# Strassen groups for all of an FFN, with the sums of its weight blocks made in DRAM

## The reference, cut to what matters

```python
h = rms_norm(x, g_pre_ffn)
x = x + rms_norm((silu(h @ w_gate) * (h @ w_up)) @ w_down, g_post_ffn)
```

## Time and profile before

| | us |
|---|---|
| median of 3 runs | 1280.83 |
| lowest and highest | 1280.55, 1282.76 |
| the profiled execution | 1281.71 |
| its span | 1279.6 |

### The profile page before, as it was taken

One profiled execution on the slowest core, in us unless ns is written; L12 is line 12 of the kernel. 1 busy time (PEld: TensorE's weight loads), 2 busy tenths in 40 slices (PEclk: granted clock), 3 DMA queues, 4 the chain that ended last, 5 costly groups with the idle time before them and its releaser, 6 DMA issues.

```text
span 1279.6 us, 16976 instructions
## 1 busy us (share of the span) xinstructions
PE 1270.1 (99%) x6329; PEld 1061.1 (83%) x6329; DVE 761.4 (60%) x1554; ACT 594.1 (46%) x1239; POOL 49.9 (4%) x97
## 2 busy tenths in 40 slices
PE   9999999999999999999999999999999999999998
PEld 8887777898888888888888888788878788999987
DVE  4366776654555455547675678675545534976664
ACT  5366676543453345335453324563335542463533
POOL 1010100100000000000100010000000000000000
PEclk9999999999999999999999999999999999999999
DMA  6279894222252236232525898212221022353531
GB/s 249 99 214 257 241 263 141 70 99 99 99 198 99 99 122 222 85 132 99 171 94 173 243 273 238 77 67 99 99 99 67 33 99 100 125 195 125 197 133 66
DMA packets 31937, 181.01 MB, mean 141 GB/s; under 512 B 3944, under 2 KB 4204, under 8 KB 12784
## 3 DMA queue, kind: packets, MB, share of 16 engines
q1 hardware_dynamic: 24360, 141.19, 31.6%
q0 software_dynamic: 4608, 33.56, 10.3%
q10 hardware_dynamic: 2888, 5.18, 1.2%
HBM read 171.52 MB, written 37.76 MB: 164 GB/s over the span
## 4 chain that ended last, share of the span: by engine, by line
PE 95%; DVE 1%; DMA 1%; issue 1%; POOL 0%; ACT 0%; ACTq 0%; POOLq 0%; SPq 0%; DVEq 0%
PE bank L2068 26%; PE bank L2070 26%; PE bank L2069 26%; PE sc L2244 3%; PE tp L2253 2%; PE ob L2268 1%; PE ob L2310 1%; PE sc L2070 1%; PE sc L2069 1%; PE sc L2068 1%; DMA act_hi<-act_hi 1%; PE bank L2185 1%; PE bank L2175 1%; PE bank L2194 1%; PE bank L2277 1%
## 5 line engine op out<-in xcount | busy, mean ns | idle before, releaser
L2068 PE MATMUL bank<-xT_hi,w_hi 128*128 128x512 f32 (+1 forms) x1040 | 407.5, 392 | 0.1
L2070 PE MATMUL bank<-xT_hi,w_lo 128*128 128x512 f32 (+1 forms) x1040 | 396.0, 381 | 0.0
L2069 PE MATMUL bank<-xT_lo,w_hi 128*128 128x512 f32 (+1 forms) x1040 | 395.6, 380 | 0.0
L1280 DVE TENSOR_TENSOR w_lo<-w_raw,w_hi 128x512 fp32r<-128x512 f32 x467 | 296.7, 686 | 165.5 <-ACT w_hi L723 163.9
L723 ACT ACTIVATE w_hi<-w_raw 128x512 fp32r<-128x512 f32 x467 | 261.3, 621 | 119.9 <-PE bank L2070 96.0
L2068 PEld LDWEIGHTS bank<-xT_hi,w_hi 128*128 128x128 f32 x1040 | 196.0, 188 | 39.5 <-issue 4.5
L2070 PEld LDWEIGHTS bank<-xT_hi,w_lo 128*128 128x128 f32 x1040 | 195.9, 188 | 38.0
L2069 PEld LDWEIGHTS bank<-xT_lo,w_hi 128*128 128x128 f32 x1040 | 196.3, 189 | 34.8 <-issue 1.2
L731 ACT ACTIVATE arena<-bank 128x512 f32<-128x512 f32 x74 | 43.8, 597 | 137.8 <-PE bank L2070 132.7
L2068 PE MATMUL bank<-w_hi,act_hi 128*128 128x512 f32 (+1 forms) x264 | 102.7, 389 | 0.0
L2070 PE MATMUL bank<-w_hi,act_lo 128*128 128x512 f32 (+1 forms) x264 | 101.1, 383 | 0.0
(11 more groups left out here) (287 smaller groups left out, 1742.2 us busy)
## 6 DMA issues: line engine op xcount, KB each, us to landing
w_raw<-in_weights SPq DMA_DIRECT2D x99, 1024.0 KB, 4.9
sum_dram<-in_weights POOLq DMA_DIRECT2D x24, 1024.0 KB, 9.5
w_raw<-sum_dram SPq DMA_DIRECT2D x16, 1024.0 KB, 4.8
sum_dram<-sum_dram POOLq DMA_DIRECT2D x8, 1024.0 KB, 8.5
...
```

The costliest lines, as they stand in the source:

```text
L1280: nc.vector.tensor_tensor(w_lo[SPLIT_AT[b]][:, cols], w_raw[SLOT[b]][:, cols], w_hi[SPLIT_AT[b]][:, cols].bitcast(F32), ALU.subtract).then ...
L2068: nc.tensor.matmul(ps, hi_l, hi_r, start=first, stop=False, skip_group_check=onto)
L2069: nc.tensor.matmul(ps, hi_l, lo_r, start=False, stop=False, skip_group_check=onto)
L2070: return nc.tensor.matmul(ps, lo_l, hi_r, start=False, stop=last, skip_group_check=onto)
```

## The change

**What it does.** Gate and up are done in groups as well: the first two chunks stay as they were (`PLAIN`), and five groups of four chunks (`up0` to `up4`) take up and gate as the two column halves of one matrix, with the input in quarters by features and tokens (`x11` to `x22`) and four forms of these (`t1` to `t4`, made once by DVE). Each group has 7 products of 48 matmuls that are 256 tokens wide. Outputs are added in three places: ACT copies products 0, 1, 3 and 5 out of PSUM, DVE adds products 2, 4 and 6 onto the copies, and ACT takes silu of the gate's. The down product becomes one group over all 22 chunks: 7 products of 11 chunks, each over three weight blocks (4, 4 and 3 chunks), accumulated in PSUM, with 512 columns and 128 tokens a matmul. The hidden values stay in one place, and DVE makes the forms `s1` to `s4` on them. POOL makes the sums of weights for eight groups of the FFN (five of up and gate, three of down) and two of the gates, now as two chains side by side, one over the even groups and one over the odd ones. `SUM_STEPS` says how many steps of each chain follow the mask of a head.

```diff
-GU = (8, 8, 6)
-QUADS = 2
-QK2 = GU[0] // 2
+PLAIN, UP_QUADS = 2, 5
+HALF_FC = FC // 2
+DOWN_CHUNKS = ((0, 4), (4, 8), (8, HALF_FC))
+N_DOWN = len(DOWN_CHUNKS)
...
+COLUMN_OPERANDS = ("11", "sum1", "12", "sum2", "pair", "22", "sum4")
+COLUMN_X = ("x11", "t1", "x21", "t2", "t3", "t4", "x22")
+FORMS = ("t1", "t2", "t3", "t4")
+X, V, Z = range(3)
+COLUMN_BANK = (X, Z, V, X, X, X, Z)
...
+ROW_OPERANDS = ("11", "21", "sum1", "22", "sum2", "pair", "sum4")
+ROW_LEFT = ("a11", "a12", "s1", "s4", "s2", "s3", "a22")
+ROW_BANK = (X, V, Z, Z, X, X, X)
...
+SUM_STEPS = [0] * 4 + [2] * 12
...
+MAKE_AT = {1: [("s1", 1), ("s2", 1)], 2: [("s1", 2)], 3: [("s2", 2)], 4: [("s4", 0)], 5: [("s4", 1)], 7: [("s4", 2)],
+           9: [("s3", 0)], 10: [("s3", 1)], 11: [("s3", 2)]}
+DOWN_ORDER = [(b, r) for b in range(N_DOWN) for r in range(2)]
+DOWN_LAST = [(0, 0), (0, 1), (1, 0), (2, 0), (1, 1), (2, 1)]
...
+                if k:
+                    pool.wait_ge(chain, 16 * 6 * k)
+                begin(s1, a1, chain)
                 yield
+                pool.wait_ge(chain, 16 * (6 * k + 1))
+                add(s1, a2, chain)
                 yield
+                if k:
+                    pool.wait_ge(pair_, 16 * 2 * k)
+                begin(pair_sum, p1, pair_)
+                pool.wait_ge(chain, 16 * (6 * k + 2))
+                begin(s2, sum_dram[s1, :, :], chain)
                 yield
+                pool.wait_ge(chain, 16 * (6 * k + 3))
+                add(s2, a3, chain)
                 yield
+                pool.wait_ge(pair_, 16 * (2 * k + 1))
+                add(pair_sum, p2, pair_)
+                pool.wait_ge(chain, 16 * (6 * k + 4))
+                begin(s4, sum_dram[s2, :, :], chain)
                 yield
+                pool.wait_ge(chain, 16 * (6 * k + 5))
+                add(s4, a4, chain)
                 yield
+            def every_second(groups):
+                for g in groups:
+                    yield from sums_of_weights(g)
+
+            weight_sums = [every_second(range(i, len(GROUPS), 2)) for i in range(2)]
+
+            def add_weights(steps):
+                step_between(weight_sums[0], steps, weight_sums[1])
+
             for h in range(HEADS):
                 pool.wait_ge(bias_loaded[h % 4], 16 * (h // 4 + 1))
                 nc.gpsimd.memset(biases[h % 4][0:CHUNK, BIAS_W - CHUNK:BIAS_W], NEG).then_inc(bias_ready, 1)
+                add_weights(SUM_STEPS[h])
...
+            add_weights(6)
+            for i in range(2):
+                pool.wait_ge(chain_summed[i], 16 * 6 * len(GROUPS) // 2)
+                pool.wait_ge(pair_summed[i], 16 * 2 * len(GROUPS) // 2)
...
+            for q in range(UP_QUADS):
+                up = FIRST[f"up{q}"]
+                if q:
+                    act.wait_ge(hidden_done, 2 * q - 1)
+                up_out(q, 0, kept(p1))
+                split(up + 2)
+                if q == 0:
+                    round_up_form("t3")
+                else:
+                    act.wait_ge(hidden_done, 2 * q)
+                up_out(q, 1, kept(p5))
+                split(up + 3)
+                if q == 0:
+                    round_up_form("t4")
+                if q == UP_QUADS - 1:
+                    round_left(0, 0)
+                split(up + 4)
+                up_out(q, 3, kept(u2))
+                split(up + 5)
+                if q == UP_QUADS - 1:
+                    round_left(0, 1)
+                split(up + 6)
+                if q == UP_QUADS - 1:
+                    act.wait_ge(up_full, 2 * (PRODUCTS * q + 5))
+                    round_left(0, 2)
+                up_out(q, 5, lambda h: up_chunks(q, h, 0), ACT.Silu, -1.0)
+                act.wait_ge(up_added, 6 * q + 4)
+                nc.scalar.activation(p5[:, :, :], p5[:, :, :], ACT.Silu, scale=-1.0).then_inc(up_silu, 1)
+                split(up + 7)
+                split(up + 8)
...
+            def up_add(q, i, dst, copied, done):
+
+                for h in range(2):
+                    dve.wait_ge(up_copied, 8 * q + copied + h + 1)
+                    dve.wait_ge(up_full, 2 * (PRODUCTS * q + i) + h + 1)
+                    nc.vector.tensor_tensor(dst[:, h, :], dst[:, h, :], up_bank[COLUMN_BANK[i]][h][:, :], ALU.add).then_inc(up_added, 1)
...
+            for q in range(UP_QUADS):
+                up, last = FIRST[f"up{q}"], q == UP_QUADS - 1
+                split(up + 2)
+                if q == 0:
+                    up_form("t3")
+                    split_up_form("t3")
+                split(up + 3)
+                if q == 0:
+                    up_form("t4")
+                    split_up_form("t4")
+                if last:
+                    split_left(0, 0)
+                split(up + 4)
+                up_add(q, 2, p1, 0, 0)
+                if last:
+                    make_left("s1", 0)
+                split(up + 5)
+                if last:
+                    split_left(0, 1)
+                    make_left("s2", 0)
+                split(up + 6)
+                up_add(q, 4, p5, 2, 2)
+                if last:
+                    split_left(0, 2)
+                for h in range(2):
+                    dve.wait_ge(up_added, 6 * q + h + 1)
+                    dve.wait_ge(up_copied, 8 * q + 6 + h + 1)
+                gated_quad(q, 0, None, p1)
+                split(up + 7)
+                split(up + 8)
+                up_add(q, 6, u2, 4, 4)
+                for h in range(2):
+                    dve.wait_ge(up_added, 6 * q + 4 + h + 1)
+                dve.wait_ge(up_silu, q + 1)
+                gated_quad(q, 1, p5, u2)
...
+            for n in range(N_DOWN * PRODUCTS):
+                j, b = n // N_DOWN, n % N_DOWN
+                if n == 18:
+                    down_add(5, p5, 2)
+                if n:
+                    split(FIRST["down"] + n + 1)
+                if n == 6:
+                    down_add(1, p1, 0)
+                if j < PRODUCTS - 1:
+                    split_left(j + 1, b)
+                for name, piece in MAKE_AT.get(n, ()):
+                    make_left(name, piece)
+                if n == 9:
+                    begin_variance("post2", 0)
+                    begin_variance("post2", 1)
+                if n == 15:
+                    down_add(3, u2, 4)
+                if n == 16:
+                    for t in range(2):
+                        gain_down(t, 0, p1[:, t, :], p1[:, t, :], False).then_inc(gained, 1)
+                    for t in range(2):
+                        gain_down(t, 1, u2[:, t, :], u2[:, t, :], True)
+                    variance("post2", 0, D)
+                    variance("post2", 1, D)
+                if n == 17:
+                    update(0)
+                    update(1)
+                if n == 18:
+                    scale("pre2", 0)
+                if n == 19:
+                    scale("pre2", 1)
+                    split_xT("pre2", 0)
...
+            def up_bank_ready(q, i, h):
+
+                if COLUMN_X[i] == "x11":
+                    pe.wait_ge(*(freed(USE["gu"] + h) if q == 0 else (up_copied, 8 * (q - 1) + 6 + h + 1)))
+                if COLUMN_X[i] == "t1" and q:
+                    pe.wait_ge(up_added, 6 * (q - 1) + 4 + h + 1)
+                if COLUMN_X[i] == "x21":
+                    pe.wait_ge(*(freed(USE["gu"] + 2 + h) if q == 0 else (up_added, 6 * (q - 1) + h + 1)))
+                if COLUMN_X[i] == "t2":
+                    pe.wait_ge(up_copied, 8 * q + h + 1)
+                if COLUMN_X[i] == "t3":
+                    pe.wait_ge(up_copied, 8 * q + 4 + h + 1)
+                if COLUMN_X[i] == "t4":
+                    pe.wait_ge(up_added, 6 * q + 2 + h + 1)
+                if COLUMN_X[i] == "x22":
+                    pe.wait_ge(up_copied, 8 * q + 2 + h + 1)
+
+            def up_quad(q):
+
+                for i, name in enumerate(COLUMN_X):
+                    where, o = COLUMN_BANK[i], FIRST[f"up{q}"] + i
+                    opens = where not in COLUMN_BANK[:i]
+                    if name in FORMS:
+                        pe.wait_ge(up_split, FORMS.index(name) + 1)
+                    moving_hi, moving_lo = (up_form_hi[name], up_form_lo[name]) if name in FORMS else (x_hi[name], x_lo[name])
+                    for h in range(2):
+                        up_bank_ready(q, i, h)
+                        for m in range(2):
+                            for k in range(KW):
+                                if h == 0 and m == 0:
+                                    pe.wait_ge(w_split, PARTS * o + k + 1)
+                                at = W * k + P * (2 * h + m)
+                                last = product(up_bank[where][h][:, ST * m:ST * m + ST], w_hi[SPLIT_AT[o]][:, at:at + P], w_lo[SPLIT_AT[o]][:, at:at + P],
+                                               moving_hi[:, k, :], moving_lo[:, k, :], opens and m == 0 and k == 0, k == KW - 1, True)
+                        last.then_inc(up_full, 1)
...
+            def down_bank_ready(j, r):
+
```

(21 more changed lines are left out.)

911 lines of the change are left out of this document (402 added, 509 removed).

## The result

| | before | after |
|---|---|---|
| median of the runs, us | 1280.69 (1279.69 to 1282.76) | 1448.77 (1446.35 to 1450.66) |
| span of the profiled execution, us | 1279.6 | 1444.6 |
| ratio to before, with its 95% interval | | 1.1309 (1.1283 to 1.1335) |

The change makes the kernel 168 us slower. The forecast was 1450 us, in a range of 1395 to 1510. The kernel before was timed again beside each set of runs, with medians from 1279.23 to 1280.69 us, so a difference between two sets is uncertain by some 1.5 us beside its own scatter.

A forecast was written before the change was run, and what follows sets the result against it. TensorE bounds the kernel before; in the changed attention, POOL's sums on full DMA engines delay the masks. 1281.71 + 147 (attention) - 19.6 + 29.5 + 4 + 8 (FFN) = 1450.6, so 1450 us by median; range 1395 to 1510.

The forecast's parts named there:

- Rival (a): Attention: POOL's chains of sums bound by full DMA engines; 1450 us, own range 1405 to 1485; chance 0.77.
- Rival (b): Attention: rounds of the two chains don't overlap, 15.1 us a round; 1510 us; chance 0.10.
- rival (c): Attention: landings take as long as before, adding 53 and 5 us; 1362 us; chance 0.08.
- Rival (d): Attention: POOL keeps pace, so only the FFN counts; 1268 us (chance 0.02) or 1304 us (0.03).
- The price of a landing: Attention: each 1 MB sum transfer takes 4.12 us of all 16 engines; 54 ahead of head 15's mask, 222.5 us.
- the two side copies: Attention: two copies of the next pair of groups, perhaps still under way at head 15's mask, not among the 54 landings.
- The two terms on top of it: After head 15: 3 us for the last two rounds ahead of the norm's square roots, 2 us for a cold PE.
- Matmuls of the FFN: FFN: removed matmuls take 325.7 us, added ones 306.1, so 19.6 us less while PE is fed.
- The new wait in each group: Up groups: product 5 waits for DVE's add behind a split, 4.2 us five times, plus 8.5 of clock: 29.5 us.
- My lower bound of 0.85: Up groups: each wait if the split were no hindrance, 0.16 of drain and 0.69 of add, 4.3 us in all.
- First group: First up group: DVE also forms t3 and t4 between its splits; 4 us, bounds 0 and 8.
- Down: Down products: product 6 waits for DVE's add behind two updates, plus clock and small waits; 8 us, bounds 2 and 16.

The follow-up runs named there:

- e1: Changed kernel without the sums of the FFN's eight groups, first quarters loaded in their place: 1306.32 us.
- e4: Changed kernel with the same 64 transfers at other times, one chain at a time, 28 steps of them beside the FFN: 1336.88 us.
- e2: Changed kernel with every add in DRAM replaced by a plain copy of the same size: 1410.65 us.
- e8: Changed kernel with one round of both chains after each of heads 4 to 15 instead of two, the rest beside the FFN: 1356.6 us.
- e7: e1 with DVE's add of product 4 ahead of the seventh split, and the down products' updates of x behind product 5's add: 1269.98 us.
- e3: Changed kernel with DVE's add of product 4 moved ahead of the seventh operand's split in each up group: 1417.74 us.
- e12: Changed kernel with sums spread, down ones one in flight, DVE's waits mended, and next weights' second part split ahead of x's third-tile update: 1289.18 us.

## Why the prediction was right, point by point

**What bounds the change: right.** Rival (a) came. POOL's masks stand behind landings, and the landings behind a full set of DMA engines. e1 shows that it is the sums, e4 that it is where they are issued, e2 and e8 that the time follows the engines' work and not a number of landings or rounds. Rival (b), 1510, and rival (c), 1362, fall with the mask at 342.61 us. Rival (d), POOL keeping pace, falls too; its 1304 us is about what e1 has without the sums, 1306.32.

**The price of a landing, and their number: right, by two small errors that cancel.** I took 4.12 us of all engines for each transfer; in the mean of the changed kernel it is 3.95, 4% less. I counted 54 landings ahead of head 15's mask and 56 had come (58.83 MB in the stretch, blocks of 1.05 MB), as the two side copies that I had left open were through. So POOL's queue took 86.7% of the 253 us from 90 to 343, 219 us against 222.5, and q1 and q10 14.7%, 37 against 35. The mask came at 342.61, forecast 347.5. That an add is dearer than a copy (e2) did no harm, since the price was a mean over both.

**The two terms on top of it (3 and 2 us): wrong, both came to nothing.** From head 15's scores to the first square root it took 30.8 us before and 29.4 after. The last two rounds were issued by then, the last transfer at 370.51 us, and POOL's idle time ahead of the root is ended by DVE. PE did come to head 15 with a low clock, 0.50 from 343 to 350 us, but it had less left to do: 124 matmuls between these two points, where there were 155 before. So the part before the FFN was 136.7 us and not 147.

**Matmuls of the FFN, -19.6: right** as far as e7 shows it. e7 stands 11.5 us under before's span (1268.1 against 1279.6), 2.8 of which is the attention without sums. The 8.7 that are left are 19.6 less the pauses still in it: six distances of 1.28 to 2.06 us, 8.7 us beyond the pitch of their matmuls, and some 2 for the clock (0.57 in 599 to 603 us).

**The new wait in each group, 29.5: right.** 4.2 us were forecast and 4.23 measured, made of the forecast's parts: a wait for ACT, 2.50 of splits, the add. The clock cost some 2.1 each and not 1.7; it fell to 0.50 behind three of them. My lower bound of 0.85 for an early add was too high: four groups of e3 have 0.26 or less, since product 5 waits only for the first half of the add, which I had overlooked. e3 puts the whole at 31.0, with the first pause's 1.3 us more in it.

**First group, 4 us: about right.** A distance of 1.44 us at 437.09, and 1.27 more in the first pause than in the others, 2.6 us without their clock.

**Down, 8 us: right in kind.** The pause ahead of the last product was 4.85 us and stood on DVE behind the two updates, as worked out. The edit of e7 took 5.3 us off; a distance of 1.85 us stayed there, and one of 1.30 at 694.74 us.

**What I had not seen: the tail of the FFN.** Behind the last down product PE stood twice, at 770.15 and 772.70 us, 1.98 and 1.93 us from matmul to matmul, waiting for `w_lo`. These 3.5 us and their clock are more than half of what the FFN is above its forecast, 28.3 instead of 21.9. I had written that the stages behind keep their order, and looked at order alone, not at how late DVE comes to it. The one reordering tried there, e12, only moved the wait.

Both errors, 10 us too much before the FFN and 6 too little in it, are small beside the 168, and they cancel in part. That the total is off by only 1.2 us is luck of that kind, and in part of another: these errors are read from a profiled execution of 1446.35 us, the fastest of the four, 2.4 us under their median.
